# The gated merge of prompt tile 0 alone ahead of the expert gathers, tile 1's by a second pass over the weights beside them

## The reference

```python
merged = jax.nn.sigmoid(parts[14]) * branch_a + jax.nn.sigmoid(parts[15]) * branch_b   # parts = h @ w_in, branch_a = hm @ w_a, branch_b = oa @ w_b
x = x + ga1 * _rmsnorm(merged @ prm['w_out'], prm['g_post1'])
h2 = _rmsnorm(x, prm['g_pre2']) * (1 + sc2) + sh2
...
    q = (hb @ wq).reshape(blk, P_HEADS, P_QDIM)                   # PEER: 8 heads
    s1, s2 = ...                                                  # scores of both query halves with 128 keys each
    v1, i1 = lax.top_k(s1, P_TOPK); v2, i2 = lax.top_k(s2, P_TOPK)
    ...                                                           # the best 16 of 16 x 16 sums: 16 experts of 16384 per token and head
    act = jax.nn.gelu(jnp.einsum('td,thkd->thk', hb, u[eidx]))
    return jnp.einsum('thk,thkd->td', (g * act), v[eidx])
```

## Time and profile before

| | us |
|---|---|
| median of 3 runs | 2362.39 (2359.65 to 2367.06) |
| the profiled execution | 2375.17 |
| its span in the trace | 2373.4 |
| Time of all 16 DMA engines, share by the software queue (the gathers and copies of POOL) | 71.8% |
| the same by SP's queue | 20.2% |
| TensorE, VectorE, ScalarE, GpSimd busy | 74%, 52%, 31%, 29% |

### The profile page before, as it was taken

How to read it: one execution, slowest core, us unless ns; L and a number is a source line. 1 busy time by engine, 2 the same in 40 slices (tenths; PEclk the granted TensorE clock), 3 DMA queues, 4 the chain that set the end, 5 groups by cost and what they waited for, 6 DMA issues and landing times.

```text
span 2373.4 us, 29093 instructions
## 1 busy us (share of the span) xinstructions
PE 1763.9 (74%) x10960; PEld 949.7 (40%) x10960; DVE 1233.9 (52%) x3177; ACT 730.1 (31%) x2191; POOL 699.7 (29%) x700
## 2 busy tenths in 40 slices
PE   8999999889999797888756556655656655555554
PEld 5777457767886454444312122212212221211111
DVE  2000011254331667666667766767676675767764
ACT  3000012222321354443343433443333322334422
POOL 0000101111020243343334344353434434443431
PEclk9999999998999899999877777777877877777777
DMA  9977859769967599999999999999999999999996
GB/s 404 358 299 304 335 194 365 269 233 379 315 215 276 222 403 419 420 420 419 388 390 420 412 383 420 419 416 419 416 418 414 419 409 411 403 420 419 421 419 276
DMA packets 126184, 875.68 MB, mean 369 GB/s; under 512 B 15792, under 2 KB 17104, under 8 KB 40284
## 3 DMA queue, kind: packets, MB, share of 16 engines
q0 software_dynamic: 85760, 691.32, 71.8%
q1 hardware_dynamic: 39332, 182.38, 20.2%
q10 hardware_dynamic: 952, 0.13, 0.0%
HBM read 861.42 MB, written 99.39 MB: 405 GB/s over the span
## 4 chain that ended last, share of the span: by engine, by line
DMA 30%; PE 16%; DVE 15%; issue 3%; ACT 2%; POOL 2%; ACTq 0%; POOLq 0%
DMA pr_ring<-in_uv,pr_idx 29%; PE ps L2073 9%; PE ps L1957 3%; DVE pr_ring L2305 3%; POOL pr_ring L1942 2%; PE ps L2003 1%; PE ps L1984 1%; DVE pr_hot L2285 1%; ACT pr_coef L2147 1%; DVE pr_hot L2289 1%; DVE pr_ind L2263 1%; DMA trunk<-in_uv,pr_idx 1%; DVE pr_ind L2260 1%; DVE pr_pick L2292 1%; PE ps L2025 1%
## 5 line engine op out<-in xcount | busy, mean ns | idle before, releaser
L2073 PE MATMUL ps<-pr_ring,pr_diag 64*64 64x512 f32 (+1 forms) x4232 | 677.3, 743 | 518.7 <-ACT pr_diag L2151 518.6
L1942 POOL DMA_INDIRECT pr_ring<-in_uv,pr_idx x556 | 605.5, 1089 | 967.1 <-PE ps L2073 794.9
L2305 DVE CUSTOM_DVE_ANT_0 pr_ring<-pr_ring,h 128x1024 f32<-128x1024 f32 x556 | 667.7, 1226 | 425.2 <-DMA pr_ring<-in_uv,pr_idx 424.2
L2073 PEld LDWEIGHTS ps<-pr_ring,pr_diag 64*64 64x64 f32 (+1 forms) x4232 | 173.8, 158 | 948.2 <-ACT pr_diag L2151 718.9
L2142 ACT ACTIVATE pr_gel<-pr_dots 128x2 f32<-128x2 f32 x288 | 58.3, 202 | 698.3 <-DVE pr_dots L2305 697.9
L2151 ACT ACTIVATE pr_diag<-fold,pr_coef 128x64 f32<-128x64 f32 x576 | 164.5, 332 | 0.0
L1957 PE MATMUL ps<-trunk,pr_wq 128*128 128x320 f32 (+2 forms) x544 | 144.4, 422 | 3.6 <-DMA pr_wq<-in_peer_wq 2.1
L2147 ACT ACTIVATE pr_coef<-pr_gel,pr_wgt 128x1 f32<-128x1 f32 x576 | 138.3, 287 | 27.8 <-ACT pr_gel L2142 1.5
L1957 PEld LDWEIGHTS ps<-trunk,pr_wq 128*128 128x128 f32 x544 | 104.5, 207 | 70.1 <-issue 41.1
L473 PE MATMUL ps<-trunk,ap_ring 128*128 128x288 f32 x384 | 126.4, 411 | 1.5 <-DVE trunk L328 1.5
L474 PE MATMUL ps<-trunk,ap_ring 128*128 128x288 f32 x384 | 124.5, 406 | 0.0
(11 more groups left out here) (318 smaller groups left out, 2116.1 us busy)
## 6 DMA issues: line engine op xcount, KB each, us to landing
out_win_s<-in_cache POOLq DMA_DIRECT2D x64, 1020.0 KB, 8.1
side_unit<-in_w_merge SPq DMA_DIRECT2D x32, 768.0 KB, 7.6
sa_ring<-in_cache SPq DMA_DIRECT2D x24, 1024.0 KB, 8.8
late_ring<-in_w_ada SPq DMA_DIRECT2D x8, 2048.0 KB, 15.4
sa_ring<-in_kcacheB SPq DMA_DIRECT2D x16, 1024.0 KB, 6.5
pr_wq<-in_peer_wq SPq DMA_DIRECT2D x16, 1024.0 KB, 9.1
out_win_s<-in_cache POOLq DMA_DIRECT2D x16, 1008.0 KB, 9.2
ap_ring<-in_w_attn_qk SPq DMA_DIRECT2D x5, 2048.0 KB, 27.9
```

The source lines that it names most:

```text
L1942: pool.indirect_dma_start(row(n), None, d["uv"], bass.IndirectOffsetOnAxis(ap=idx[:, b % 4, j:j + 1], axis=0)).then_inc(arrived[slot(n)], 16)
L2073: mm = pe.matmul(ps[half * TS:(half + 1) * TS, bank + t, :], diag[tokens, slot(n), :], row(n)[tokens, o:o + CHUNK], start=h == 0 and j == ...
L2305: ins = dve.tensor_tensor_reduce(u, u, e.h2[:, BLOCKS[b][0], :], 1.0, 0.0, ALU.mult, ALU.add, dots[:, slot(n):slot(n) + 1])
```

## The change

1. In `mlstm_and_merge` a unit has 128 columns (tile 0) in place of 256. Two units in succession share one sigmoid, one multiplication and one addition of 256 elements a row. Fourteen of the 16 units stand in the chunks' loop (`BEFORE_SUMS`, `AFTER_SUMS`), unit 14 behind it and unit 15 behind the third state update. The stores of the states are no longer waited for in this block: SP (before unit 10's load) and POOL (before gather 6) wait for them in the next one.
2. In `output_and_experts` tile 0's `w_out` product comes first, alone. Tile 1's merge is a second pass over the same 16 units (`unit1`), four units to one PSUM bank (`quad_sigmoid`, `quad_merged`): units 0 to 2 behind tile 0's product, 3 to 7 behind its first scores, 8 between two queries, 9 to 15 in steps 0 to 6 beside the gathers. Eight of these units are loaded into ring slots (`RING_HOME`), which the gathers get as the units are used. Tile 1's `w_out` product stands in steps 8 and 9, its normalisation and turn in steps 11 to 13.
3. The ring has 8 slots for the first 24 gathers, then 10 (the ninth of the ring and the memory of `merged`, which is free once tile 1's product is made: gather 24 waits for it), and 12 from gather 456 on.
4. The blocks begin with tile 0's heads 0, 1, 2, then tile 1's 2, 1, 0, then both tiles in turn. The query weights are loaded for 18 rounds in place of 16. All 16 units of the rest run beside the gathers, from step 12 on, in place of 14 from step 2 on.

```diff
-    before_sums = lambda c: 2 * c - 1
-    after_sums = lambda c: 2 * c
-    TAIL = 2 * LAST + 1
+    BEFORE_SUMS = ((), (2, 3), (6, 7), (10,), (12,))
+    AFTER_SUMS = ((0, 1), (4, 5), (8, 9), (11,), (13,))
+    TAIL, FINAL_UNIT = 14, 15
...
-                sp.wait_ge(s_out, 32)
                 sp.wait_ge(m.s_new, 16)
...
-                        if n == 0:
+                        if n < len(FIRST_FREED):
+                            pool.wait_ge(s_unit, FIRST_FREED[n] + 1)
+                        if n == OWN - 2:
+                            pool.wait_ge(front.s_states, 32)
+                        if n == JOINED:
                             pool.wait_ge(s_mm, GROUP)
...
                 for n in range(2):
                     pe.wait_ge(front.s_w[n], 32)
-                    product(0, n, 0, KD)
-                product(1, 0, 0, KD)
-                product(1, 1, 0, KD // 2)
+                    product(0, n)
+                for u in range(3):
+                    unit1(u)
                 turn(0)
-                product(1, 1, KD // 2, KD)
...
+                for u in range(3, 8):
+                    unit1(u)
+                query(2)
+                unit1(8)
+                query(3)
                 scores(1)
+                pe.wait_ge(s_quad_add, 2)
...
+                        if g < UNITS1 - UNITS_BEFORE:
+                            unit1(UNITS_BEFORE + g)
+                        if g in (FIRST_PRODUCT1, FIRST_PRODUCT1 + 1):
+                            pe.wait_ge(s_quad_add, 4)
+                            product(1, g - FIRST_PRODUCT1)
```

More of the change, by code:

```diff
@@ L1618, in _ @@
                     ins.then_inc(s_tt, 1)
[L1619 to L1620 removed]
+                mg.sigmoid(act, FINAL_UNIT)
             @block.vector
@@ L1697, in _ @@
                     ins.then_inc(s_sc, 1)
-                    mg.take(dve, TAIL + 1 + h)
-                for t in range(TAIL + 1 + H, mg.UNITS):
-                    mg.take(dve, t)
+                    if h == 2:
+                        mg.take(dve, FINAL_UNIT)
 GROUP = 2
@@ new lines, with pieces_for, piece_place @@
+ROUND_START = [[r for r, *_ in PIECES].index(at) for at in range(len(ROUNDS))] + [len(PIECES)]
+def pieces_for(i, h):
+    tile = tile_cols(i)
+    return 1 + max(n for n, (_, head, _, span) in enumerate(PIECES)
+                   if head in ((h,) if i < PT else (h, h + PH // 2)) and span.start <= tile.start < span.stop)
+def piece_place(n):
+    r, h, half, span = PIECES[n]
+    if h == ALONE - 1 and span == TILE0:
+        return 2 + half
+    if span == TILE1:
+        return 13 + half + (0, 4, 8)[ALONE - 1 - h]
+    if span == OTHERS and h == 0:
+        return 112 + half
+    slow = 2 * (h if span == BOTH else PH + h) - 3
+    return PER * slow + 4 + 2 * half
@@ L1783, in slot @@
 def slot(n):
-    return n % RING if n < GROWN else (n - GROWN + RING) % WIDE
-def in_front(n):
-    return n - RING if n < GROWN else n - WIDE if n >= GROWN + WIDE else n - WIDE if n >= GROWN + 2 else -1
-def arrivals(n):
-    return sum(slot(m) == slot(n) for m in range(n + 1))
+    return SLOT[n]
 def output_and_experts(nc, k, d, e, front):
@@ L1866, in query_of, with unit_tile @@
             return e.first[:, f % 4, i % GROUP * P:(i % GROUP + 1) * P]
+        def unit_tile(u):
+            if u in RING_HOME:
+                return ring[:, RING_HOME[u], 0:(KD + H) * P].rearrange("p (c n) -> p c n", n=P)
+            return front.unit[:, side_home(u)[0]]
         with nc.Block() as block:
@@ L1980, in first_scores, with product @@
                         pe.sem_inc(s_sc, 1)
[L1982 to L1984 removed]
+                def product(i, n):
+                    for c in range(KD):
+                        mm = pe.matmul(ps[:, out_bank(i) + n, :], front.merged[:, i, c, :], front.w[:, n, c, :],
                                        start=c == 0, stop=c == KD - 1)
[L1986 removed]
+                    if n == 1:
                         mm.then_inc(s_mm, 1)
```

505 lines of the change are left out of this document (305 added, 200 removed).

## The result

The changed kernel takes 2371.93 us in the median of six runs (2367.29 to 2375.07, and one of 3000.44 in which TensorE's clock was 0.549 and which is left out of the ratio), the kernel before 2360.54 us beside it (2358.63 to 2367.06). The ratio is 1.0041 with a 95% interval of 1.0027 to 1.0056: slower by 9.7 us, where 12 us less were predicted.

What follows compares the result with a forecast made beforehand. Compute up to the first gather was taken to set the pace, then full DMA from 798 to 2358 us. Terms: -31 - 2 + 0 + 16 + 5 = -12, from 2362.4 to 2350 us; range 2336 to 2366.

Steps and rivals of the forecast that it cites:

- Term 1: Tail of the mLSTM block, from the sample states' products to the block's end: ends at 723.0 instead of 753.9, -31 us.
- Term 2: mLSTM chunk loop: fourteen half units for nine whole ones, -8 us, against load stalls of +6: -2, between -8 and +3.
- Term 3: Output block's start to first gather: rows 3 us late, first query 2.2 us sooner, about 0 (-2 to +13).
- far bound of 13: Before the first gather: up to 13 us more if six unit loads share time with store and rows; not taken.
- Term 4: Full DMA stretch beside the gathers: 6.55 MB more at 415 GB/s, with no cover, +16 us.
- Term 5: First gathers with 8 ring slots: gather 24 waits for tile 1's output product, +5 us, bounds 0 and 16.
- upper bound of 16: Gather 24's wait: the most DMA idle time allowed for, 16 us.
- some 5 us of the 15.7 are idle: Gather 24's wait of 15.7 us: about four outstanding gathers and two or three weight loads leave DMA idle some 5 us.
- Rival (b): First gathers: TensorE and VectorE starve DMA, deciding from 20 us idle; at 25 us idle +8, or 2370 us; chance 0.15.
- sign of being wrong: First 100 us of gathers: DMA share below 0.95; also, rest or query weight loads holding up TensorE in the full stretch.
- The mapping to the median: Whole kernel: the median lies 12.8 us below the profiled execution, before and after the change alike.
- near 763: Sign in the new trace: the first gather goes out near 763 us, where before it came at 796.44.

Runs made afterwards that it cites:

- refill: Changed kernel with unit 14's gate product issued three times, filling TensorE's pause before the state updates: 2365.72 us, ratio 0.9999.
- cut pair: Kernel before and changed kernel, both cut off where the mLSTM block ends, without the states' store and two nearby loads: 747.98 and 729.91 us.
- fewbytes: Changed kernel with the loads of second-pass units 11 to 15 and the rest's first two units cut to 1 of 12 row blocks: 2377.24 us, ratio 1.0026.
- join32: Changed kernel with the memory of `merged` entering the ring at gather 32 instead of 24, the last two slots at 454: 2378.72 us, ratio 1.0044.
- noprod: Changed kernel with tile 1's output product cut to 1 of 8 weight tiles for each half: 2363.39 us, measured once.
- spread: Changed kernel with tile 1's product in quarters over steps 8 to 11, its later work two steps later, ring as in join32: 2370.97 us, ratio 1.0011.
- ring8: Kernel before with only the changed kernel's ring plan (8 slots, 10 from gather 24, 12 from 456): 2370.61 us, ratio 1.0012.
- c_before: Kernel before, unchanged, timed and traced a second time: 2368.68 us, ratio 0.9999.
- c2_before: Kernel before, unchanged and whole, timed and traced once more: 2369.64 us, ratio 0.9999.
- head_before: Kernel before, cut off where the mLSTM block ends, without the 2 MB states' store and two loads behind it: 747.98 us.

## Why the prediction was wrong, step by step

**Term 1, the tail, -31: mis-sized.** By the first pair of traces it is -22.9, by the later ones -21. The order and the counts were right, the durations not: I priced every row behind 709.5 at the full clock. Against refill, whose tail takes 13.6 us in place of 21.9, L1585 took 0.8 us more, the updates 1.8 and 3.5 (7.14 for eight, 3.65 in refill), the turn 0.2, unit 15 1.8 and 0.3, 8 us in all. The pause of 4.01 us that precedes them was in my own text ("still waits for VectorE, as unit 9's does", 0.29 us in the earlier trace rows). The units in front of it are half as long, so the same chain on VectorE leaves TensorE 3.7 us more of waiting. The sum allowed for that time, since term 2 counts no gain for the unit that this chain covers; what it did not allow for is that the work behind such a wait runs slower. The Trainium skill (TensorE: Matmul & The Clock Gate, HAM oscillation) says that idle gaps let the array's clock fall to 1.2 GHz, so that the work behind a gap runs cold, and asks to arrange the work without such gaps. The trace agrees for this pause (a granted clock of 0.50 from 705 to 715), and refill agrees with the remedy. Gaps are not all of it here: the unit at 712.51 of the kernel before ran slow with no idle time in front of it, and the first query of the changed kernel behind waits of only 1.5 and 1.1 us.

**Term 2, the loop, -2: right** in the profiled pair (-1.9), but no fixed size. The stalls came as expected: six waits for `sa_ring`, together 5.5 us, and one of 2.03 for `side_unit`. The traces of before contain waits of their own of 1.2 to 3.9 us there, though, and slow spots. So the stretch is shorter by 1.9, 2.2 and 6.0 us in the three pairs of whole traces and longer by 3.2 in the cut pair, where before ran at a clock of 1.00. What decides in one execution how long these waits are and how often the clock falls was not found.

**Term 3, block start to first gather, 0: right in size** (-0.9), with parts that cancel otherwise than in the sum. The rows landed 11.3 us after their issue at 724.0, in time: VectorE starts 15.6 us behind the block's start in both kernels, so the 3 us of lateness did not come. The 2.2 us ahead of the first query were won. The first query at half speed cost 1.7 us. The far bound of 13 did not come either. The Trainium skill (DMA: Bandwidth & Descriptors, Queues, rings and completion order) has descriptors consumed in ring order on each DMA engine; the 11.3 us, with the six units issued right behind the rows, agree with that, and no run here has the units ahead of them.

**Term 4, bytes, +16, "has no cover": the bytes right, the cover wrong for a part.** 6.63 MB more were moved. But fewbytes took 5 MB of them away and won nothing in the trace: where the engines set the pace, bytes and idle time lie in the same microseconds. As a sum over the whole stretch, bytes by rate and idle time still add up to about what was lost (16 + 16 for 28 to 30); as prices of single edits they don't.

**Term 5, the first gathers, +5: mis-sized, the largest error.** Between 65 and 100 us behind the first gather, DMA moved 222 GB/s x 35 us = 7.8 MB in the changed kernel and 419 x 35 = 14.7 MB in the kernel before: 6.9 MB or 16.5 us at 419 GB/s, just above the upper bound of 16 that I had given. In the 65 us ahead of it and the 65 us behind it the two differ by +1 and -1 MB. I had the mechanism (gather 24 behind the product), and the wait of 19.0 us against 15.7. What failed is "some 5 us of the 15.7 are idle": of the two or three weight loads that should have covered the wait one is there at most, since SP issues the last at 833.40, before POOL begins to wait, and the next at 890.61, when the first unit of the rest has been used; and the 9.5 us wait at 827.60, behind the third route, had already taken the lead of the gathers. join32 shows that the memory's wait is not the cause, noprod that the product is (11 us), spread that its two lumps are (10 us, or 8 beside join32).

**Rival (b), 0.15,** came nearest: slower, with some 17 us idle in the first 100 us, by the shares 0.97 and 0.69 of the two halves. That is a mean of 0.83, below the 0.95 that I had named as the sign of being wrong, and short of the 20 us from which this rival was to decide; the rest of the miss lies ahead of the gathers, which it left as forecast. Its counter-argument, totals of 65 and 75 us of work in 80 us of traffic, said nothing of the order: a total hides a lump. ring8 speaks against the part of the rival that blamed the 8 slots: by themselves they cost nothing.

**The mapping to the median.** I took the difference between one profiled execution and the median (12.8 us) for both kernels. Later profiled executions of before lay 5.3 us above their median, those of the changed kernel between 1.9 below and 1.9 above. The granted clock goes with this: the three profiled executions of before have means of 0.862 to 0.863, where the 24 runs of c_before and c2_before have a median of 0.867; their runs at 0.872 and above took 2359 to 2363 us, and those at 0.862 and 0.863 took 2371 to 2375. In the five runs of head_before the longest (753.6) has 0.970 and the shortest (744.3) 0.982. No run sets the clock apart as the cause. One pair of profiled executions was then worth -3.8 us, of which -5.8 lay in unchanged code. For the same reason it is luck that the first gather came at 764.90 where I had written "near 763": counted from L1012 it came after 180.8 us, where the sum gave 173.6. From the cut kernels' means the sum closes: -19.5, one more for the cut (estimated), -0.9 for the stretch up to the first gather, and the gathers' stretch from the means of three traces each, 1605.9 - 1576.2 = +29.7, give +8; measured were +7.8, +8.3 and +9.7 by the ratios. Of the 20 us between forecast and result, rounded, 9 lie behind the first gather (29.7 for 21: 11 more of idle time, some 3 less than bytes and idle time add up to) and 12 ahead of it (21.4 won for 33). The slow clock behind the pause is 8 of these by the rows, and 3 to 8 by the filled pause; the rest is the quicker loop of before in the timed runs, which fits its higher clock there but stays open.

## What to carry to other kernels

When work is moved under a full DMA stretch, compare its longest uninterrupted piece on the engine that frees the buffers, plus what stands behind it, with what is outstanding, and count no load as cover without looking up when it is issued; cut the piece before touching the memory it waits for. When merge work is thinned out, carry over each wait that it used to hide, and price what stands behind a new pause of TensorE of some 4 us at half clock. Before believing a difference of some 5 us between two profiled executions, subtract what lies ahead of the first changed instruction, compare their granted clocks, and time the cut-off head by itself, both versions on the same chip.

## What the runs showed of the hardware

Repeating a product of 2.0 us twice more made the kernel faster: with TensorE working through a pause of 4.0 us the first state update took 1.96 us in place of 3.76 in all three versions, and the ratio to the kernel before fell from 1.0033 to 0.9999. The clock also fell where TensorE had hardly been idle: a query behind waits of 1.5 and 1.1 us took 3.68 us in place of 1.95, and a unit with none in front 5.41 in place of 3.72. Identical code ahead of L1012 took 581.2 to 591.8 us in the traces of all kernels here, and the runs of one whole kernel spread over 12 to 23 us, while the stretch from the first gather to the end, some 1576 and 1606 us long, repeated within 3 us in the three traces of each kernel.
